# Moving the shared scratch region of a two-block transformer kernel by 128 bytes

## The reference

```python
def first_block(x, mem, ...):
    x = x + 0.5 * swiglu(rms_norm(x, g), w_gate, w_up, w_down)      # width 2816
    z = rms_norm(x, g) @ w_in                                       # 7 parts of 512 columns
    o_h = hgrn2_chunkwise(q, 1 - f, zi, log(f))                     # gated linear recurrence, 4 heads of 128
    y_conv = zb * causal_depthwise_conv(zc * zu, conv_w)            # 3 taps
    x = x + concat(rms(o_h) * silu(zg), y_conv) @ w_out
    x = x + softmax_attention(rms_norm(x) @ w_q, rms_norm(mem) @ w_kv) @ w_o   # 256 memory rows, 4 heads
    x = x + 0.5 * swiglu(rms_norm(x, g), w_gate, w_up, w_down)
    return rms_norm(x, g)

def second_block(x, ...):
    proj = rms_norm(x) @ w_in                                       # 5120 columns
    ya = moba_attention(...)                                        # 8 heads of 64, ALiBi bias
    yb = diff_attention(...)                                        # 4 heads, difference of two softmaxes
    merged = sigmoid(ga) * (ya @ w_a) + sigmoid(gb) * (yb @ w_b)
    x = x + rms_norm(merged @ w_out)
    return x + rms_norm((silu(h @ w_gate) * (h @ w_up)) @ w_down)   # h = rms_norm(x), width 2816
```

## Time and profile before

| | |
|---|---|
| Median of the runs | 1957.02 us (1956.5 to 1958.78) |
| The execution that was profiled | 1958.78 us |
| Its span, first to last instruction | 1957.1 us |
| PE busy | 1916.0 us, 98% |
| DVE busy | 908.2 us, 46% |
| ACT busy | 705.5 us, 36% |
| POOL busy | 176.8 us, 9% |
| HBM traffic | 89 GB/s over the span |
| Mean granted clock of TensorE | 0.991 |

### The profile page before, as it was taken

How to read it: one execution, slowest core, us unless ns; L and a number is a source line. 1 busy time by engine, 2 the same in 40 slices (tenths; PEclk the granted TensorE clock), 3 DMA queues, 4 the chain that set the end, 5 groups by cost and what they waited for, 6 DMA issues and landing times.

```text
span 1957.1 us, 24117 instructions
## 1 busy us (share of the span) xinstructions
PE 1916.0 (98%) x9630; PEld 1559.2 (80%) x9630; DVE 908.2 (46%) x1182; ACT 705.5 (36%) x957; POOL 176.8 (9%) x150
## 2 busy tenths in 40 slices
PE   8999999998999999999999999999999989999998
PEld 6888888887778898888888878777667868888887
DVE  6444432447685654644443246343546454444313
ACT  5222221354534443522222143334545453222212
POOL 2000000205330200200000032000000030000000
PEclk9999999999999999999999999999999989999999
DMA  5333322232214223333322222111212323333222
GB/s 162 97 96 97 96 97 94 99 108 66 66 44 151 86 87 108 86 104 89 103 90 104 89 89 87 65 65 44 69 61 86 94 57 93 101 92 101 90 104 75
DMA packets 213697, 175.79 MB, mean 90 GB/s; under 512 B 6565, under 2 KB 201210, under 8 KB 213626
## 3 DMA queue, kind: packets, MB, share of 16 engines
q1 hardware_dynamic: 212928, 174.74, 29.1%
q10 hardware_dynamic: 698, 0.05, 0.0%
HBM read 172.67 MB, written 2.10 MB: 89 GB/s over the span
## 4 chain that ended last, share of the span: by engine, by line
PE 88%; DVE 5%; ACT 3%; POOL 2%; issue 1%; DMA 1%; SPq 0%; DVEq 0%; POOLq 0%; ACTq 0%
PE bank L484 25%; PE bank L486 24%; PE bank L485 24%; PE bank L658 6%; PE bank L531 2%; PE bank L951 1%; PE bank L532 1%; PE bank L533 1%; ACT w_hi L1049 1%; PE bank L920 1%; DVE w_lo L1511 1%; DMA w_raw<-in_w_in 1%; PE bank L935 1%; DVE n_lo L1520 1%; POOL sum_squares L425 0%
## 5 line engine op out<-in xcount | busy, mean ns | idle before, releaser
L484 PE MATMUL bank<-n_hi,w_hi 128*128 128x512 f32 x1760 | 707.9, 402 | 18.0 <-DVE n_lo L1520 9.5
L1511 DVE TENSOR_TENSOR w_lo<-w_raw,w_hi 128x2048 fp32r<-128x2048 f32 x160 | 369.1, 2307 | 744.4 <-ACT w_hi L1049 744.3
L486 PE MATMUL bank<-n_hi,w_lo 128*128 128x512 f32 x1760 | 690.9, 393 | 0.0
L485 PE MATMUL bank<-n_lo,w_hi 128*128 128x512 f32 x1760 | 690.5, 392 | 0.0
L1049 ACT CAST w_hi<-w_raw 128x2048 fp32r<-128x2048 f32 x160 | 305.4, 1909 | 600.9 <-PE bank L486 519.0
L484 PEld LDWEIGHTS bank<-n_hi,w_hi 128*128 128x128 f32 x1760 | 333.4, 189 | 103.4 <-issue 24.0
L486 PEld LDWEIGHTS bank<-n_hi,w_lo 128*128 128x128 f32 x1760 | 333.2, 189 | 71.1
L485 PEld LDWEIGHTS bank<-n_lo,w_hi 128*128 128x128 f32 x1760 | 333.8, 190 | 68.2 <-issue 2.6
L425 POOL TENSOR_TENSOR sum_squares<-sum_squares,sq 128x512 f32<-128x512 f32 x42 | 65.9, 1569 | 927.4 <-ACT sq L1064 923.0
L484 PE MATMUL bank<-h_hi,w_hi 128*128 (+1 forms) x352 | 137.1, 390 | 0.2
L486 PE MATMUL bank<-h_hi,w_lo 128*128 (+1 forms) x352 | 136.9, 389 | 0.0
(11 more groups left out here) (306 smaller groups left out, 1953.7 us busy)
## 6 DMA issues: line engine op xcount, KB each, us to landing
w_raw<-in_w_in SPq DMA_DIRECT2D x68, 512.0 KB, 4.6
w_raw<-in_ffn_gate SPq DMA_DIRECT2D x44, 512.0 KB, 4.1
w_raw<-in_ffn_up SPq DMA_DIRECT2D x44, 512.0 KB, 5.2
w_raw<-in_ffn_down SPq DMA_DIRECT2D x44, 512.0 KB, 3.9
w_raw<-in_w_gate SPq DMA_DIRECT2D x22, 512.0 KB, 4.1
w_raw<-in_w_up SPq DMA_DIRECT2D x22, 512.0 KB, 5.2
w_raw<-in_w_down SPq DMA_DIRECT2D x22, 512.0 KB, 4.2
w_raw<-in_w_kv_mem SPq DMA_DIRECT2D x16, 512.0 KB, 4.4
```

The source lines that it names most:

```text
L484: pe.matmul(acc, w_hi, x_hi, start=start, stop=False)
L485: pe.matmul(acc, w_hi, x_lo, start=False, stop=False)
L486: return pe.matmul(acc, w_lo, x_hi, start=False, stop=stop)
L1511: dve.tensor_tensor(wlo[par][:, :], raw[par][:, :], whi[par][:, :].bitcast(F32), ALU.subtract).then_inc(w_lo_ready, 1)
```

## The change

One line, the one that sets where the arena starts.

```diff
         masks = sb("level_masks", [P, 6, 32], I32)
         maskt = sb("mask_tmp", [P, 3, 32], I32)
-        arena = -(-(cursor[0] - 128) // 1024) * 1024 + 128
+        arena = -(-cursor[0] // 64) * 64
         arena_size = nc.sbuf_usable_end - arena
```

## The result

The change made the kernel slower by half a per cent: 1970.22 us at the median (1967.21 to 1971.44, four runs) beside 1957.9 us (1956.5 to 1958.86, four runs), a ratio of 1.0051 with the 95% interval 1.0039 to 1.0063. The ratio is not the quotient of these two medians: over all eighteen executions of the changed kernel on record, 1965.1 to 1971.44 us, the median is 1967.2, about 10 us above before, and the four alone overstate the loss. (The ratios further down can differ in the same way from the quotient of the medians beside them, by up to 0.001.) The profiled execution took 1967.05 us, its span is 1965.3 us, 8.2 us longer than before. The forecast of no change was wrong, and the time lies outside its range.

A forecast was written before the change was run, and what follows sets the result against it. The prediction took PE's matmul pace to bound the kernel, with a matmul under way for 1916.0 of 1957.1 us. All terms were 0, giving 1957.0 us for the median, range 1954.2 to 1959.5 us.

The forecast's parts named there:

- The failed step: Matmuls over 512 columns with an arena operand, 1824 of them: 0 ns each, bounds -24 to +24 us.
- rival C: Recurrence and second block's attention shift in time, changing clock stretches and waits: 1952 to 1962 us; chance 0.10.
- The sign of being wrong: A group with an arena operand has another median by more than 2 ns while groups on fixed tiles have not.
- Rival B: Down projections and merged layer: moving and weight reads disturb each other without common remainder, 1981 us; chance 0.04.
- rival S: Named in the experiments: a start on a multiple of 256 costs by itself, about 2003 us in e1; no chance given.
- the term's own upper bound of +24 us: Matmuls with an arena operand: largest difference between groups of this form, 13 ns, for 1824 matmuls.
- Rival A: Matmuls with an arena operand lose 13 ns each once it starts on a boundary: 1933 us; chance 0.03.
- The other terms: Instructions, helper engines on arena tiles, DMAs, clock: 0 each; helpers within 0.7 us, DMAs -0.4 to 0, clock within 1.7.
- the DMA account: DMAs of x_tok into the arena: 17 blocks become 16, last landing 0.4 us sooner; taken at 0.

The follow-up runs named there:

- e4: Changed kernel with h_hi and h_lo (and x_tok_a behind them) put back by 128 bytes: 1958.19 us, ratio 1.0007.
- e5: Kernel before with h_hi and h_lo (and x_tok_a) moved down by 128 bytes: 1965.33 us, ratio 1.0038.
- e3: Separate kernel of 31 matmul-only sections, varying d, moving operand's start address less stationary one's, by remainder of 256: 226.7 ns at 0, 233.4 at 0/128.
- e6: Kernel before with the whole arena moved up by 256 bytes: 1957.4 us, ratio 0.9999.
- e7: Matmul-only kernel like e3, 31 more sections with other address differences, narrower weights and fewer moving columns: 226.7 to 240.0 ns across differences at 512 columns.
- e8: Matmul-only kernel like e3, 55 sections with the remaining multiples of 4 bytes: none under 226.7 ns at 512 columns; 113.3 to 123.4 at 256.
- e12: Kernel before with mem_hi and mem_lo alone 64 bytes lower: 1956.05 us, ratio 0.9991.
- e2: Kernel before with x, n_hi, n_lo and arena moved to 256 above a multiple of 1024, weights staying at 128: 1991.14 us, ratio 1.0163.
- e1: Kernel before with fixed tiles and arena both starting 256 bytes above a multiple of 1024: 1955.7 us, ratio 0.999.
- e13: Matmul-only kernel, 21 sections in a dense layer's sequence, some in other orders: 226.7 ns at difference 0, 233.3 and 236.7 at 240.

## Why the prediction was wrong

*The failed step* is the one on the matmuls with an operand in the arena, taken at 0 ns for each. In steps under 300 ns, where PE makes no pause, it is 6.6 ns at L484 to L486 (226.7 before, 233.3 after) and 5.6 ns at L658 (226.8 before, 232.4 after). The count was right but for 48: those on `att_pt_hi` have both operands in the arena, so d stayed 0, and they still take 390 ns. For the other 1776 that makes 11 us; by stages the trace shows 3.5 + 3.3 us in two down projections, 2.8 us in the last and 1.2 us in the merged layer (its `merged_hi` row spans 44.1 us for 42.9), 10.8 us. The span grew by less, 8.2 us, since the recurrence ran 1.8 us shorter (see rival C) and 0.7 us was made up after the merged layer. e4 takes the loss away and e5 brings most of it back, alone. The sign of being wrong that the prediction named came as well: 394 for 389 ns with `h_hi` and `merged_hi`, and `n_hi` at 389.

*Rival B* had the right cause and the right place: the down projections and the merged layer slow down once the regions lose their common remainder. (That it is two reads that disturb each other is taken up under what stays open.) It had a chance of 0.04 and twice the true price, 13 ns. Three readings led there. First, the prediction held against it that the offset is 0 or 512 bytes by turns and that the shortest and the median matmul do not differ for it. That is true, but e3 and e6 show a period of 256, so 0 and 512 are one case, and the trace held no second one. Second, L739 as evidence: both its operands step together, so d is 0 there too, and it has 32 columns. It spoke against rival S of the experiments, not against B. Third, equal paces in the earlier trace rows show only that arena and fixed region are alike at d = 0. All rows cited as evidence shared the one thing that the change took away. The range was too narrow for the same reason: the term's own upper bound of +24 us was worked out and then left out as unlikely, without a row in which the relation was other than 0.

*Rival A* is out: after the change the arena operand does start on a boundary, and the pace rose. Nor is the 13 ns over 512 / 2.4 GHz something an offset takes away; no multiple of 4 bytes did in e3, e7 and e8.

*The other terms held.* L1575 takes 693 ns for 692, L1111 620 for 621. `x_tok` landed after 3.6 to 6.4 us for 3.6 to 6.5, so the 0.4 us of the DMA account do not show as more than 0.1. The mean clock was 0.991 in both, with 0.88 from 512 to 526 us again. *Rival C*: the recurrence ran 1.8 us shorter in the one profiled execution, with less waiting before L706, 3.3 us for 4.9. That is of the size that C allowed, but the change is not needed for it. From the split at 389 us to the one at 566 the time is 176.9 us before and 175.1 after; of the two runs that leave the recurrence's tiles where they were before, e5 has 177.0 us and e12 175.0. What decides it was not looked into.

The Trainium skill, "SBUF — State Buffer", section "SBUF: two separate sides", has contention as a matter of ports, and its section "A bandwidth-pool intuition that's wrong" gives TensorE a second, independent read port for weight loads. The prediction had cited the first under rival A, and called the equal paces an agreement with it; those paces were all at d = 0. The measurement differs from it: with all other engines idle, a matmul of TensorE cost 226.7 to 240.0 ns by the difference of its two operands' addresses (e3, e7, e8).

*What stays open.* That the weight load of the next matmul and the moving stream of this one are the reads that collide is an inference. It fits that both directions count and that no other engine is needed, but no run removed the weight loads. The rule of the cost is open: it is not one value for each difference (240: 226.7, 233.3 and 236.7; d = 112 and 128 moved as well, and the kernel's own `h` matmuls at 128 have 233.3 in the changed kernel, 232.9 in e2 and 232.4 in e5), and narrower weights did not lower it. What was seen as constant is d = 0 at 512 columns and weights of 128, in each section and kernel once it had settled.

## What to carry to other kernels

Where matmuls run back to back, look at where moving and stationary tiles start before calling a layout change free: here a common remainder by 256 was worth 0.5% of the kernel in three down projections and one more layer, and 1.6% when all activations lost it (e2). Keep the tiles of all matmuls over 512 columns, in all regions, at one remainder by 256, as both the kernel before and e1 do. And when a trace is to show that something has no effect, ask first whether the thing varies in it at all; if it does not, the bound of the term belongs in the range.

## What the runs showed of the hardware

At none of 64 differences did a section of fp32r matmuls over 512 columns settle at a mean step under 226.7 ns, which is 544 cycles of 2.4 GHz; the slowest means were 240.0 ns, 576 cycles. Over 256 columns d = 0 is one of the worst cases, 120.0 ns, and 16 or 192 gave 113.3, so the best offset depends on the shape. Weights of 32 columns instead of 128 made a matmul over 512 columns no faster, 231.6 for 226.7 ns. And a section of 48 equal matmuls can settle at another pace than the same code elsewhere, 240 being the case seen twice at the same addresses (233.3 and 236.7 ns, e13), so one section is not enough to price an offset other than 0.
